# Feed-forward output passes over 4, 8, 6 and 4 tiles, x parked in DRAM, sums moved to VectorE, norm roots inverted in turned blocks

## What is computed

```python
def swiglu(x, w_gate, w_up, w_down):            # D_FF = 2816 = 22 tiles of 128
    a = einsum('btd,df->btf', x, w_gate)
    b = einsum('btd,df->btf', x, w_up)
    return einsum('btf,fd->btd', silu(a) * b, w_down)

for l in range(2):
    g = norm_g[l]
    ff_a = swiglu(rms_norm(x, g[0]), ...)
    x = x + 0.5 * rms_norm(ff_a, g[1])
    mix = mixer(rms_norm(x, g[2]))              # l = 0: two attentions, l = 1: one
    x = x + rms_norm(mix, g[3])
    ff_b = swiglu(rms_norm(x, g[4]), ...)
    x = x + 0.5 * rms_norm(ff_b, g[5])
```

## Time and profile before

| | |
|---|---|
| median of 3 runs | 1890.29 us (1889.52 to 1898.1) |
| profiled execution: its time | 1890.94 us |
| profiled execution: its span | 1889.1 us |
| instructions in the span | 38834 |
| matmuls | 15552 |
| granted TensorE clock, mean | 0.997 of full speed |

### The profile page before, as it was taken

The page is one execution under the profiler, slowest core; times in us unless marked ns, Lnnn a source line. Parts: engine busy times, 40 slices in busy tenths (PEclk is TensorE's granted clock), DMA queues, the critical chain, the costliest instruction groups (busy, mean ns, idle before and its releaser), DMA issues.

```text
span 1889.1 us, 38834 instructions
## 1 busy us (share of the span) xinstructions
PE 1871.0 (99%) x15552; PEld 1820.7 (96%) x15552; DVE 1546.1 (82%) x2030; ACT 1182.5 (63%) x2281; POOL 303.9 (16%) x317
## 2 busy tenths in 40 slices
PE   9999999999999999999999999999999999999997
PEld 9999999999669999999999999999997999999997
DVE  7889998698773888999868799997767487999975
ACT  7666666765684656666676666666738555656564
POOL 0002020300362100202020002020335200020202
PEclk9999999999999999999999999999999999999999
DMA  4232322322311122322231223233241222232322
GB/s 163 90 107 96 107 96 92 124 72 102 126 46 46 60 98 90 100 103 96 100 129 46 101 95 107 91 111 103 99 125 42 71 68 101 84 118 85 116 90 72
DMA packets 59042, 177.95 MB, mean 94 GB/s; under 512 B 7072, under 2 KB 11504, under 8 KB 58736
## 3 DMA queue, kind: packets, MB, share of 16 engines
q1 hardware_dynamic: 55504, 166.50, 26.0%
q0 software_dynamic: 2128, 7.80, 1.3%
q10 hardware_dynamic: 1232, 1.16, 0.2%
HBM read 168.26 MB, written 5.36 MB: 92 GB/s over the span
## 4 chain that ended last, share of the span: by engine, by line
PE 94%; DVE 2%; ACT 2%; issue 1%; POOL 1%; DMA 0%; ACTq 0%; POOLq 0%; DVEq 0%
PE psum L929 29%; PE psum L927 29%; PE psum L928 29%; PE psum L1292 1%; PE psum L1278 1%; PE psum L1411 1%; PE psum L1200 1%; PE psum L1394 1%; PE psum L1366 1%; PE psum L1255 1%; PE psum L1244 0%; DVE xlo L2311 0%; DMA x<-in_x 0%; ACT w_hi L730 0%; DVE y L2222 0%
## 5 line engine op out<-in xcount | busy, mean ns | idle before, releaser
L927 PE MATMUL psum<-xhi,w_hi 128*128 128x272 f32 x1552 | 451.6, 291 | 1.6 <-DVE xlo L2311 1.5
L929 PE MATMUL psum<-xhi,w_lo 128*128 128x272 f32 x1552 | 448.1, 289 | 0.0
L928 PE MATMUL psum<-xlo,w_hi 128*128 128x272 f32 x1552 | 446.6, 288 | 0.0
L927 PEld LDWEIGHTS psum<-xhi,w_hi 128*128 128x128 f32 x1552 | 292.5, 188 | 5.1 <-issue 2.6
L928 PEld LDWEIGHTS psum<-xlo,w_hi 128*128 128x128 f32 x1552 | 292.5, 188 | 0.5
L929 PEld LDWEIGHTS psum<-xhi,w_lo 128*128 128x128 f32 x1552 | 291.8, 188 | 0.0
L780 DVE TENSOR_TENSOR w_lo<-w_raw,w_hi 128x1024 fp32r<-128x1024 f32 (+1 forms) x208 | 236.7, 1138 | 64.8 <-ACT w_hi L777 62.2
L928 PE MATMUL psum<-corner,w_hi 128*128 128x272 f32 x864 | 250.1, 289 | 0.0
L929 PE MATMUL psum<-corner,w_lo 128*128 128x272 f32 x864 | 250.0, 289 | 0.0
L927 PE MATMUL psum<-corner,w_hi 128*128 128x272 f32 x864 | 248.9, 288 | 0.0
L777 ACT ACTIVATE w_hi<-w_raw 128x1024 fp32r<-128x1024 f32 (+1 forms) x208 | 206.2, 991 | 40.0 <-PE psum L929 38.5
(11 more groups left out here) (363 smaller groups left out, 4937.9 us busy)
## 6 DMA issues: line engine op xcount, KB each, us to landing
w_raw<-in_w_gate_up SPq DMA_DIRECT2D x172, 512.0 KB, 4.2
w_raw<-in_w_down SPq DMA_DIRECT2D x96, 384.0 KB, 3.6
w_raw<-in_w_down SPq DMA_DIRECT2D x32, 256.0 KB, 2.8
w_raw<-in_even_in SPq DMA_DIRECT2D x16, 512.0 KB, 3.7
w_raw<-in_odd_in SPq DMA_DIRECT2D x10, 512.0 KB, 4.2
w_raw<-in_even_out SPq DMA_DIRECT2D x8, 512.0 KB, 3.4
w_raw<-in_odd_out SPq DMA_DIRECT2D x8, 512.0 KB, 4.1
out_band_kv<-qkvb POOLq DMA_DIRECT2D x1, 2176.0 KB, 9.8
```

The costliest lines, as they stand in the source:

```text
L927: nc.tensor.matmul(out, s_hi, m_hi, start=first, stop=False, skip_group_check=skip)
L928: nc.tensor.matmul(out, s_hi, m_lo, start=False, stop=False, skip_group_check=skip)
L929: return nc.tensor.matmul(out, s_lo, m_hi, start=False, stop=last, skip_group_check=skip)
```

## The change

- The folded output passes take 8 and 6 tiles in place of 6 and 6, and the last pass takes 4 in place of 6. `fold` 0 to 3 now stand after `seven` 8, `fold` 4 to 7 after `seven` 14. Three `seven` steps are left behind them in place of five.
- For room, the high parts of the fold's sums (`fold_hi`) and one gate lie in the place of x. x is stored to the output tensor y in DRAM after the last `gain`, by SP ahead of the `first` weight loads, and read back by SP ahead of the `last` weight loads.
- The three sums that GpSimd made in each fold are made on VectorE: its `sum_fold` goes, and one of that name comes on VectorE.
- `reciprocal` turns 256 of the 272 columns in blocks of 32 by 32, inverts one column of each of the 8 blocks and the 16 columns left over, and turns the 8 columns back, each read 32 times. (All 128 partitions hold the same row.)
- One strided VectorE instruction over two sums of h becomes two.

```diff
-PASS = 6
-FOLDED = 6
+PASSES = (8, 6)
+LAST = KF - PLAIN - sum(PASSES)
+FOLDED = sum(PASSES) // 2
+LATE = (PASSES[0] // 2 - 1, FOLDED - 1)
-STEPS = [("seven", q) for q in range(7)] + [("fold", j) for j in range(4)] + [("seven", q) for q in range(7, 13)] + \
-    [("fold", j) for j in range(4, 8)] + [("seven", q) for q in range(13, SEVEN)]
+STEPS = [("seven", q) for q in range(9)] + [("fold", j) for j in range(4)] + [("seven", q) for q in range(9, 15)] + \
+    [("fold", j) for j in range(4, 8)] + [("seven", q) for q in range(15, SEVEN)]
...
+        x_at = cursor[0]
         x = place("x", [P, KD, T], F32)
-        fold_hi = place("fold_hi", [P, 3, 3, TH], F32R, at=h_at + 4 * T * PASS)
+        fold_hi = place("fold_hi", [P, 4, 3, TH], F32R, at=x_at)
+        gate_apart = place("gate_apart", [P, 2, T], F32, at=x_at + 4 * 12 * TH)[:]
...
                     for j, (what, i) in enumerate(KINDS["ffn"]):
+                        if (what, i) == ("first", 0):
+                            sp.wait_ge(gained, KD * (n + 1))
+                            sp.dma_start(outs["y"], x[:]).then_inc(x_kept, 16)
+                        if (what, i) == ("last", 0):
+                            sp.wait_ge(x_kept, 16 * (n + 1))
+                            sp.wait_ge(product_done, product_event(s, STEPS.index(("fold", FOLDS - 1)), "T4"))
+                            sp.wait_ge(pair_ready, len(PAIRS) * n + PASSES[0] // 2 + 1)
+                            sp.dma_start(x[:], outs["y"]).then_inc(x_back, 16)
                         for u in range(2):
...
-                    last_tiles(s, i, range(PASS - 2))
+                    last_tiles(s, i, range(LAST - 2))
                 pe.wait_ge(pair_lo, len(PAIRS) * (n + 1))
                 for i in range(4):
-                    last_tiles(s, i, range(PASS - 2, PASS))
+                    last_tiles(s, i, range(LAST - 2, LAST))
...
             def fold_high(s, p):
                 act.wait_ge(fold_made, 3 * (FOLDED * ffn_no(s) + p) + 3)
+                if p == 0:
+                    act.wait_ge(x_kept, 16 * (ffn_no(s) + 1))
...
             def reciprocal(c, post, H):
                 dve.wait_ge(std_ready, std_event(c, post, H) + 1)
-                own_wait(own(nc.vector.reciprocal(rstd[:, HALF[H]], rstd[:, HALF[H]])))
+                most, rest = slice(H * TH, H * TH + 256), slice(H * TH + 256, (H + 1) * TH)
+                one = turned[:, 0:1]
+                first = bass.AP(one.tensor, one.offset, [one.ap[0], [32, 8], [1, 1]])
+                again = bass.AP(one.tensor, one.offset, [one.ap[0], [32, 8], [0, 32]])
+                last = own(nc.vector.transpose(turned[:], rstd[:, most]))
+                nc.vector.reciprocal(rstd[:, rest], rstd[:, rest])
+                own_wait(last)
+                own_wait(own(nc.vector.reciprocal(first, first)))
+                own_wait(own(nc.vector.transpose(rstd[:, most], again)))
             def update(c, H, split_after=None):
...
+                if after_ffn(c):
+                    dve.wait_ge(x_back, 16 * (ffn_no(c - 1) + 1))
...
+            def sum_fold(s, k, part):
+                j, n, before = STEPS[k][1], fold_no(s, k), 4 * step_no(s, k)
+                m = 2 * (j % 4) + 1
+                mid, corner = partial[k % 2][:, 0, :], partial[k % 2][:, 1, :]
+                if part == 0:
+                    if j == 0:
+                        dve.wait_ge(first_read, 2 * KD * (ffn_no(s) + 1))
+                    dve.wait_ge(kept, before + 3)
+                    nc.vector.tensor_tensor(corner, corner, y[:, m, HALF[1]], ALU.add).then_inc(fold_summed, 1)
+                    nc.vector.tensor_tensor(mid, mid, y[:, m, HALF[0]], ALU.add).then_inc(fold_summed, 1)
+                    return
+                dve.wait_ge(kept, before + 4)
+                dve.wait_ge(fold_summed, 3 * n + 1)
+                nc.vector.tensor_tensor(y[:, m, HALF[1]], corner, scratch[:, 3, :], ALU.add).then_inc(fold_summed, 1)
...
                         else:
+                            sum_fold(s, k - 1, 1)
                             add_fold(s, k - 1, "B22")
                             add_fold(s, k - 1, "T4")
...
                     if kind == "fold":
+                        sum_fold(s, k, 0)
                         add_fold(s, k, "B21")
...
-                nc.vector.tensor_tensor(made, both, twice, ALU.subtract).then_inc(fold_made, 1)
+                nc.vector.tensor_tensor(left21, left21, left11, ALU.subtract)
+                nc.vector.tensor_tensor(sum2, sum1, left11, ALU.subtract).then_inc(fold_made, 1)
```

More of the change, by code:

```diff
@@ L111, in split_pair @@
     made = made_pair(k)
-    if made in (2, 5) or made is not None and made >= FOLDED:
+    if made in LATE or made is not None and made >= FOLDED:
         return made
     before = made_pair(k - 1) if k > 0 and STEPS[k][0] == STEPS[k - 1][0] == "seven" else None
-    return before if before is not None and before < FOLDED and before not in (2, 5) else None
+    return before if before is not None and before < FOLDED and before not in LATE else None
 def std_event(c, post, H):
@@ L548, in pair_tiles, with fold_place, last_tile @@
         def pair_tiles(p):
-            return slice(2 * (p % 3), 2 * (p % 3) + 2)
+            first = 2 * (0, 1, 2, 3, 0, 1, 2, 3, 0)[p]
+            return slice(first, first + 2)
+        def fold_place(p):
+            return p if p < PASSES[0] // 2 else p - PASSES[0] // 2
+        def last_tile(k):
+            return pair_tiles(FOLDED + k // 2).start + k % 2
         def gate_of(p):
-            return gate_apart if p in (3, 6) else h_gate[:, pair_tiles(p), :]
+            return gate_apart if p == PASSES[0] // 2 else h_gate[:, pair_tiles(p), :]
         def fold_factor(name, l):
@@ L608, in width_of @@
         def width_of(k):
-            return (4 if STEPS[k][0] == "seven" else 3) * P
+            kind, j = STEPS[k]
+            return (4 if kind == "seven" else PASSES[j // 4] // 2) * P
         def step_no(s, k):
@@ L880, in _ @@
                                 m = 2 * (i % 4) + u
-                                at = (PLAIN + PASS * (2 if what == "last" else i // 4)) * P
-                                load(G0[s] + j, u, ins["w_down"][n, m][:, at:at + PASS * P], PASS * P)
+                                part = 2 if what == "last" else i // 4
+                                at, width = (PLAIN + sum(PASSES[:part])) * P, (PASSES + (LAST,))[part] * P
+                                load(G0[s] + j, u, ins["w_down"][n, m][:, at:at + width], width)
                 else:
@@ L2005, in ffn_act @@
                     before = made is not None and made != made_pair(k)
-                    late = made in (2, 5)
+                    late = made in LATE
                     if before:
@@ L2430, in fold_sums @@
                 left11, left21, left12, left22 = (h_raw[:, i, HALF[H]] for i in (t, u) for H in range(2))
-                sum1, sum2, sum4 = (fold_raw[:, p % 3, i, :] for i in range(3))
-                apart = (2 * PASS + 3 * (p % 3) - 2 * t - 1) * TH
-                both = bass.AP(left21.tensor, left21.offset, [left21.ap[0], [apart, 2], left21.ap[1]])
-                made = bass.AP(left21.tensor, left21.offset, [left21.ap[0], [apart + TH, 2], left21.ap[1]])
-                twice = bass.AP(left11.tensor, left11.offset, [left11.ap[0], [0, 2], left11.ap[1]])
+                l = fold_place(p)
+                sum1, sum2, sum4 = (fold_raw[l][:, i, :] for i in range(3))
                 dve.wait_ge(pair_ready, len(PAIRS) * ffn_no(s) + p + 1)
@@ L2493, in ffn_dve @@
                         sums(dve, s, k + 1)
-                    if made is not None and made < FOLDED and made not in (2, 5):
+                    if made is not None and made < FOLDED and made not in LATE:
                         fold_sums(s, made)
@@ L3047, in layouts @@
     a["w_gate_up"] = np.stack(gu, 2)
-    halves = [at + t for at in (PLAIN, PLAIN + PASS) for e in range(2) for t in range(e, PASS, 2)]
-    tiles = list(range(PLAIN)) + halves + list(range(PLAIN + 2 * PASS, KF))
+    halves = [PLAIN + sum(PASSES[:i]) + t for i in range(2) for e in range(2) for t in range(e, PASSES[i], 2)]
+    tiles = list(range(PLAIN)) + halves + list(range(KF - LAST, KF))
     a["w_down"] = c(i["ffn_w_down"].reshape(4, KF, P, KD, P)[:, tiles].transpose(0, 3, 2, 1, 4)).reshape(4, KD, P, KF * P)
```

67 lines of the change are left out of this document (27 added, 40 removed).

## The result

The changed kernel takes 1926.24 us (median of 4 runs, 1925.26 to 1934.17), against 1889.9 for the kernel before beside it: ratio 1.0195, interval 1.0179 to 1.0211. It is slower by some 36 us; 1924 was forecast, 1905 to 1941 the range. The profiled execution took 1925.26, its span is 1923.2, 34.1 above that of before.

What follows compares the result with a forecast made beforehand. TensorE, busy 99% of the span, was taken to bound the kernel. 1890.94 plus 23.9 for shorter last passes (products and inversions included) plus 9.7 for the store gave 1924.5, stated as 1924; range 1905 to 1941.

Steps and rivals of the forecast that it cites:

- Products: Each feed-forward: 96 products fewer in the last pass, 84 more in folds 0 to 3; 1.5 us less, four times 6.0.
- The last pass: Feed-forwards with a layer behind: the shorter pass gains 4.2 of 12.1 us; 7.3 slower each, three such 21.9.
- The last feed-forward: No x to write and no weights to split behind it, so only the first waits stand: 2.0 us slower.
- The store: Feed-forward starts: first weight loads come late behind the store of x; TensorE loses 2.8, then 2.3 each, 9.7 in all.
- The line: SP's queue: weight loads issued behind the store wait for it in ring order; without that, 1915.
- The inversions: Norm roots: 1.1 us in place of 1.85, 24 times; without this gain 7 us more in all.
- Sums on VectorE, read back: Folds: three sums, 1.3 us a fold, covered by products; reading x back, 8.6 us, hidden too; cost nothing.
- The loads do not pass the store: Rival at the starts: loads pass the store or are needed later, only the last pass costs; 1915, chance 0.2.
- The covers did not hold: Rival in the last pass: nothing waits for ScalarE's chain or the store, only products and inversion count; 1884, chance 0.1.
- The clock did fall: Rival: TensorE's clock falls at the wait before result 14, up to 1929, or the store is slow, 1934; chance 0.13.

Runs made afterwards that it cites:

- e5: Changed kernel, with ScalarE taking results 10 and 11 of the last pass before it waits for the next x: 1925.40 us, ratio 1.0168 to 1.0200.
- e9: Changed kernel, with the store of x issued from ScalarE's queue after a wait for the last gain: 1922.32 us, ratio 1.0127 to 1.0182.
- e4: Changed kernel with the old single inversion of 272 columns in place of the turned one: 1932.71 us, ratio 1.0199 to 1.0246.
- e8: Kernel before, with only the fold sums moved to VectorE: 1891.66 us, ratio 1.0005.
- e11: Changed kernel with passes back at 4, 6, 6, 6 tiles and the store behind the loads of the first two groups: 1887.27 us, ratio 0.9980.
- e1: Changed kernel, with the store of x and its wait for the gains moved behind the first two groups of loads: 1916.12 us, ratio 1.0133.
- e10: Changed kernel, store behind the first two groups of loads, root and results ahead of most of ScalarE's next-layer weight splits: 1923.65 us, ratio 1.0120 to 1.0181.

## Why the prediction was right, step by step

- *Products:* right. The stretches A grow by 84 products each, and the last passes shrink.
- *The last pass:* right, almost row by row; the waits themselves were a little shorter than said. The last pair cost 0.80 and the near weights ahead of it 0.29 of idle time (1.4 forecast), result 6 0.16 (0.4). Forecast against the start of the pass: half sum wanted and late, until p 19.0; measured 368.25 - 349.28 = 18.97, a wait of 1.27 (1.6). Inversion at 23.2; 372.40 is 23.12. Bank of result 14 at 28.4, a wait of 3.4; 377.71 is 28.43, with 3.32. Last low part at 34.9:

```profile
371.90 0.47 ACT L1742 ACTIVATE rstd<-psum,eps 128x272 f32<-128x272 f32 x1
...
375.63 0.93 ACT L1760 ACTIVATE xhi<-x,gains 128x272 fp32r<-128x272 f32 x2 [2.31 <-DVE x L2269]
...
377.26 0.40 ACT L1921 ACTIVATE psum<-y 128x272 f32<-128x272 f32 x1
...
383.68 0.52 DVE L2349 SCALAR_TENSOR_TENSOR xlo<-x,gains,xhi 128x272 fp32r<-128x272 f32 x1 [0.42 <-ACT xhi L1760]
```

  It ends at 384.20, p 34.92. These are the answers to the earlier trace rows. That the boundary would not be shorter without the wait for the bank was argued there and is shown by e5: the low parts then cost as much. What TensorE waits for last in the changed kernel is the sum for half 1, in feed-forward 2:

```profile
1389.55 0.39 PE L1191 MATMUL psum<-total_hi,ones 128*128 128x272 f32 x1 [1.05 <-POOL total_lo L2954]
```

  That is p 37.8, as 387.08 is in feed-forward 0; before it was p 41.0 (377.39 - 336.36), so it comes 3.2 sooner, as said. Each boundary gave back 3.33 us of 12.1 (58.22 to 54.89) where 3.3 was forecast (4.2 less 0.9), so a feed-forward with a layer behind it is 7.2 slower; 7.3 was said.
- *The last feed-forward:* mis-sized. 2.0 slower was said; 10.6 less the tail's 7.6 is 3.0. Most of the difference is the wait for the sum of half 1, in the changed kernel and before:

```profile
1912.53 0.39 PE L1191 MATMUL psum<-total_hi,ones 128*128 128x272 f32 x1 [2.01 <-POOL total_lo L2954]
```

```profile
1877.76 0.39 PE L1166 MATMUL psum<-total_hi,ones 128*128 128x272 f32 x1 [0.39 <-POOL total_lo L2899]
```

  It grew by 1.6, where the step allowed 0.9: 0.7 of the 1.0.
- *The store:* the mechanism was right, the term 9.7 mis-sized; that 9.5 came out is luck. The tile came 8.4 to 9.0 after the gain (9.4 said, from 8.6 for a store that took 7.7). The store itself costs 2.8 in feed-forward 2, as said, but 2.0, 1.4 and 1.3 in the others, not 2.3: 7.5. The 2.0 at the first of the wider folds was not foreseen, since VectorE's work in the folds was put at nothing; it made 9.5 of it.
- *The line:* only half of it. The loads do stand behind the store on SP's queue, as the 1.5 KB of the earlier trace rows suggested; but e9 shows that a queue of their own would not have freed them.
- *The inversions:* 1.20 for 1.1. What they save was put at 7 in all; e4 shows 7.7 (4.0 at the starts, 2.6 at the boundaries, 1.1 in the tail), of which its median shows 6.5.
- *Sums on VectorE, read back:* nothing, as said (e8, e11). The read took 10.7, not 8.6, and stayed hidden, though that is longer than the step of 10.6 that the prediction gave as its bound.
- *The rivals.* The loads do not pass the store: e1 shows what that would have given, 1916 (1915 was worked out). The covers did not hold. The clock did fall behind the wait for result 14, in feed-forwards 0 and 1 and not in 2 (windows of the changed kernel, feed-forward 0; the number behind the five engines is PEclk):

```profile
375.00:379.00 4.00, 1.29 (x8) 1.29 (x9) 4.00 (x7) 3.33 (x9) 1.10 (x2) 0.92 0.13 52
379.00:383.00 4.00, 4.00 (x24) 4.00 (x24) 4.00 (x7) 3.04 (x9) 2.19 (x3) 0.65 0.00 0
```

  At 0.65, a part of these 4 us ran at 1.2 GHz in place of 2.4. The pass is 33.08 us long with the fall, 31.99 without it in feed-forward 2, and yet it cost nothing: B is 54.89 and 54.87, since the sum for half 1 was late anyway, by 0.40 with the fall and 1.05 without. A fall that the sum does not cover costs, as in e10. The Trainium skill (TensorE: Matmul & The Clock Gate, "HAM oscillation — how this bites in real kernels") warns of such falls behind gaps; here they came behind two waits of 3.32 out of three, and did not decide.

## What to carry to other kernels

A pass that only TensorE limits is also the cover of everything that must be ready behind it; count what the cover hides before moving work out of it. Here 96 products left each last pass, 84 came back elsewhere at full price, and of the 12.1 us only 3.3 were real at each of three boundaries.

The largest wait that a profile names need not be the cost. Removing it shows what is late next, and a timeline of the other engines tells that beforehand.

A large transfer set ahead of small urgent ones holds them up: here the first came 8.4 us after its issue in place of 2.7, and 6.0 with the large one on another queue at the same moment. Behind them it cost nothing, nor from the other queue 3.2 us sooner.

## What the runs showed of the hardware

The attention's stretch C takes 280.9, 282.5, 284.1, 285.7 or 290.2 us in the profiled executions (to 0.1): the first four in steps of 1.6 us, which is what one fall of TensorE's clock cost by the earlier trace rows. The edits do not explain it: 280.9 comes with either form of the inversion (e1, e4), and e8 and the kernel before, at 290.2 and 282.5, differ in the folds alone. Two windows of e1, which had no fall, and of e8, which had most, over the same work (88 us from the start of C):

```profile
490.00:510.00 20.00, 18.57 (x167) 9.88 (x166) 12.56 (x21) 12.78 (x34) 4.50 (x3) 1.00 0.37 115
510.00:530.00 20.00, 20.00 (x271) 11.96 (x269) 16.74 (x29) 14.44 (x37) 9.78 (x8) 1.00 0.01 2
```

```profile
482.00:502.00 20.00, 18.57 (x152) 9.69 (x150) 11.91 (x20) 11.73 (x30) 4.31 (x3) 0.89 0.38 114
502.00:522.00 20.00, 20.00 (x172) 11.22 (x168) 9.43 (x15) 8.31 (x27) 5.82 (x5) 0.60 0.01 2
```

TensorE is as busy in both, and idle for the same 1.43 us; the clock granted is 1.00 in the one and 0.89 and 0.60 in the other. What makes a fall come or not in one execution was not tried and stays open. It is worth up to 9 us here, as much as most of the edits.

The same 2.2 MB take 7.7 us out to DRAM and 10.7 back, both as one DMA on SP's queue; that queue carries weight loads as well, and no run tells apart what the way back shares with them.
